# Gate and up projections of the SwiGLU units 1 to 9: tokens stationary instead of weights, and the gated products transposed back on TensorE

## The chip, the cores and the metric

One NeuronCore of a Trainium2 chip runs the whole program; the other cores are idle. The metric is the device time of that core in microseconds, the median of the runs of one kernel. Two changes of a few microseconds are told apart on a program of 2.2 ms only if the runs are close together, so differences of about 0.3% are the limit of what can be read.

## The reference, cut to what matters

The program computes two mixer layers and then four layers of attention and SwiGLU, for 256 tokens of width 1024, in fp32. The change lies in the SwiGLU of the last four layers:

```python
D_FF = -(-8 * D_MODEL // (3 * 256)) * 256          # 2816
def swiglu(h, w_gu, w_down):
    g, u = jnp.split(h @ w_gu, 2, axis=-1)
    return (jax.nn.silu(g) * u) @ w_down
def second_block(...):
    for i in range(DEPTH_2):                        # 4 layers
        ...
        h = modulate(rmsnorm_2(x, norm_gain[i, 1]), sh2, sc2)
        x = x + g2[:, None, :] * swiglu(h, ffn_w_gu[i], ffn_w_down[i])
```

The modulation vectors come from `c_act @ ada_w[i]`, a large weight for a single row, which the kernel computes on VectorE while other work goes on.

## The kernel before, in words

**Three products for one.** Every fp32 operand of a large product is split in two fp32r parts, `hi` and `lo`. `three` issues hi x hi, hi x lo and lo x hi into one accumulation; each has its own weight load.

**The weight stream.** All weights pass in one fixed order through 8 buffers `raw` of 128x1024 fp32, in pieces of 256 rows x 512 columns. SyncE issues the transfers (`h_piece`), each once its buffer was read. ScalarE rounds a piece to `whi` (`h_split`), VectorE takes the difference as `wlo` (`h_rest`). `refill` keeps five split pieces ahead in the code, so in VectorE's queue the rest of a piece stands about four pieces before its use on TensorE. Between them stand pieces of `ada_w`, each multiplied with `c` and added up on VectorE (`h_ada`); most of them fall in the SwiGLU of the second block's layers 0, 1 and 2, and none in that of layer 3. Every fourth of them is followed by four transposes and sums (`ada_sums`). All engines work their queue strictly in the order that the program wrote.

**A SwiGLU layer** (`ffn`) goes through the 2816 hidden columns in 11 units of 256. A unit takes four pieces (`gemm`, K = 1024, columns of gate and of up side by side) and gives the activated product of 256 hidden columns for 256 tokens; two pieces of `w_down` (`down`) then add its share to the output, in four banks of PSUM.

**Unit 0** (`ffn_head`, `h_gu0`) has tokens as stationary operand: a bank holds 128 tokens x (256 gate, 256 up). ScalarE takes tanh of the gate half, VectorE two steps of 256 columns (gated, times up). Its product has tokens on the partitions, and `w_down` needs hidden columns there, so `act_T`, put in `deferred` and taken out by `gemm` after the second piece of the next unit, transposes it with four 128x128 transposes on TensorE (`h_gu0_tr`), and splits it to `OT.hi` on ScalarE and `OT.lo` on VectorE (`h_split_tr`).

**Units 1 to 10** have modes "FF": the weights are stationary and the 256 tokens move, 96 matmuls of 256 columns each. Bank 0 gets the gate, bank 1 the up half, with hidden columns on the partitions, which is what `down` needs. `h_gu`: tanh of 512 on ScalarE, two steps of 512 on VectorE, `OT.hi` on ScalarE, and `OT.lo` on GpSimd (in unit 10 on VectorE).

**The order of a layer**: gemm(v), down(v-1), gemm(v+1), down(v), and so on; unit 8 to 10 of `w_down` are partly held back for the layer's end (`cross`), where the residual, the norm and the next head are interleaved. There are four banks G for the units; two are held by a gemm, one is taken by a transposition, one by the sums of `ada_w`.

Of the kernel before, what the change touches and what calls it, by code (L numbers as in the profile page):

```python
# [7 lines left out]
F32 = mybir.dt.float32  # L8
F32R = mybir.dt.float32r
ALU = mybir.AluOpType  # L10
# [4 lines left out]
D = 1024  # L15
# [410 lines left out]
class Order:  # L426
# [34 lines left out]
    h_gu = h_down = h_down1 = h_last_gain = h_last_rows = h_end = h_none  # L461
# [1519 lines left out]
        self.cross(first, second, N, R, self.ffn_head(l), True)  # L1981
        gb.release(N.nx[0] + N.nx[1])

    def ffn_head(self, l):

        act, made = self.mk_blk(2), []
        self.ffn0 = act, made

        def ev(t, ps, full):
            tmp = self.mk_blk(2)  # L1990
            tanh, gated, u = self.new("ac_ev"), self.new("ve_ev"), self.new("ve_ev")
            self.h_gu0(ps, tmp, act.a[:, t * 256:t * 256 + 256], full, act.w, tanh, gated, u)
            tmp.release([u])
            made.append(u)
            return [u]
        return self.apart(self.HT, ("gu", l, 0), ev)

    def ffn(self, l):
        M, OT = self.M, self.OT
        acc_free = self.slots[0].ps_free + self.slots[1].ps_free  # L2000
        act, made = self.ffn0

        def act_T():
            g, tr = self.gbank(), self.new("pe_tr")
            self.h_gu0_tr(g, act, made, self.gfree[g], tr)
            act.release([tr])
            hi, lo = self.new("ac_tr"), self.new("ve_tr")
            self.h_split_tr(OT.hi[:, 0:2, :].rearrange("p a c -> p (a c)"), OT.lo[:, 0:2, :].rearrange("p a c -> p (a c)"),
                            M.GB[g][:, :], 1.0, tr, OT.waits(0, 2), hi, lo)
            self.gfree[g] = [lo]  # L2010
            OT.write(0, 2, [lo])
        self.deferred.append(act_T)

        def down(v):
            b0 = 2 * (v % 4)
            for kc in range(1 if v == 8 else 2):
                n, lo = self.take(("dn", l, v))
                used = ("pe_w", n)
                self.h_down(b0 + kc, n % NSPL, lo, acc_free if v == 0 and kc == 0 else [], v == 0 and kc == 0, used)
                self.give(n, used)  # L2020
                OT.free[b0 + kc] = [used]

        for v in range(1, 11):
            b0 = 2 * (v % 4)
            tmp = self.mk_blk(4)
            keep = {}

            def ev(g, ps, full):
                if g == 0:
                    keep["g"] = self.new("ve_ev")  # L2030
                    self.h_gu(0, ps[:, :], full, tmp, self.new("ac_ev"), keep["g"], None, None, None, None, False)
                    return [keep["g"]]
                u, hi, lo = self.new("ve_ev"), self.new("ac_ev"), self.new("ve_ev" if v == 10 else "po_ev")
                self.h_gu(1, ps[:, :], full, tmp, None, keep["g"], u, (b0, OT.waits(b0, 2)), hi, lo, v == 10)
                OT.write(b0, 2, [lo])
                keep["r"] = [lo]
                return [u]
            self.gemm(self.HT, 0, ("gu", l, v), D, "FF", ev)
            tmp.release(keep["r"])
            if v == 6:  # L2040
                gb = self.mod_row(l, 40)
            if v == 7 and l in (0, 1):
                w = M.I[("gla_w_in_2", "fox_w_in_2")[l]][0][:, 3072:3088]
                self.narrow_load(w, ("w16a", "w16b")[l])
                if l == 1:
                    self.selb = self.mk_blk(1)
                    self.tsel = self.load("POOL", "sel", self.selb.a[:, 0:16], M.C["foxsel"], self.selb.w)
            if v == 9 and l in (0, 1):
                self.w16[1]()
                if l == 1:  # L2050
                    self.h_sel(self.selb, self.tsel, ("ac_mask", "sel"))
                    self.selb.release([("ac_mask", "sel")])
            if v == 8:
                N = self.modulated(l + 1, 0) if l < 3 else Norm(self, self.row_gain("fn", M.I["final_norm_2"]))
            if v < 10:
                down(v - 1)

        ws = {}
        R = [[Resid(self, gb, u, t, lambda u=u, t=t: M.AB[t][:, u, :], N) for u in range(2)] for t in range(2)]

        def freed(t, u, free):
            self.slots[t].ps_free = free if u == 0 else self.slots[t].ps_free + free

        def part(t, v, u):
            def f():
                for kc in range(v == 8, 2):
                    if (v, kc) not in ws:
                        ws[(v, kc)] = self.take(("dn", l, v))
                    n, lo = ws[(v, kc)]
                    b = 2 * (v % 4) + kc  # L2070
                    done = ("pe_dn", (l, t, v, u, kc))
                    self.h_down1(t, (u,), b, n % NSPL, lo, v == 10 and kc == 1, done)
                    if t == 1 and u == 1:
                        self.give(n, done)
                        OT.free[b] = [done]
                R[t][u].full, R[t][u].free = done, lambda free: freed(t, u, free)
            return f
        if l < 3:
            head = (self.swa_head, self.gla_head, self.fox_head)[(l + 1) % 3](l + 1)
            first = [part(0, v, u) for v in (8, 9) for u in range(2)]  # L2080
            first += [part(0, 10, 0), R[0][0].all, part(0, 10, 1), R[0][1].all]
            second = [part(1, v, u) for v in (8, 9) for u in range(2)] + [part(1, 10, 0)], [], [part(1, 10, 1)]
            self.cross(first, second, N, R, head, False)
            gb.release(N.nx[0] + N.nx[1])
            return None
        yb = self.mk_blk(8)
        stored, tgain = [], self.new("ve_n")
        self.h_last_gain(N.A, tgain)
        for t in range(2):
            F = dict(s=self.smc(2), w=self.smc(6), tmp=[], sq=[], x=[])  # L2090
            for v in (8, 9):
                for u in range(2):
                    part(t, v, u)()
            for i in range(2):
                for kc in range(2):
                    if (10, kc) not in ws:
                        ws[(10, kc)] = self.take(("dn", l, 10))
                    s, lo = ws[(10, kc)]
                    done = ("pe_dn", (l, t, 10, i, kc))
                    self.h_down1(t, (i,), 4 + kc, s % NSPL, lo, kc == 1, done)  # L2100
                    if t and i:
                        self.give(s, done)
                        OT.free[4 + kc] = [done]
                self.last_part(t, i, gb, yb, done, F)
            for u, d in enumerate(self.last_rows(t, N.A, tgain, yb, F)):
                stored.append(self.load("SP", f"out{t}{u}", M.out[0][t * P:t * P + P, u * 512:u * 512 + 512],
                                        yb.a[:, t * D + u * 512:t * D + u * 512 + 512], [d]))
        return stored
# [510 lines left out]
class ScalarE(Order):  # L2619
# [124 lines left out]
            e.wait_ge(*self.at(t))  # L2744
        e.activation(tmp.a[:, 0:256], ps[:, 0:256], ACT.Tanh, scale=0.5).then_inc(*self.up(tanh))

    def h_gu(self, part, ps, full, tmp, tanh, gated, u, dst, hi, lo, end):
        e, OT = self.e, self.OT
        if part == 0:
            e.wait_ge(*self.at(full))  # L2750
# [4 lines left out]
        b0, free = dst  # L2755
# [159 lines left out]
class VectorE(Order):  # L2915
# [289 lines left out]
            e.wait_ge(*self.at(t))  # L3205
        e.scalar_tensor_tensor(act, g, 0.5, ps[:, 256:512], ALU.mult, ALU.mult).then_inc(*self.up(u))

    def h_gu(self, part, ps, full, tmp, tanh, gated, u, dst, hi, lo, end):
        e, OT = self.e, self.OT
        g, up = tmp.a[:, 0:512], tmp.a[:, 512:1024]  # L3210
        if part == 0:
# [5 lines left out]
        for t in tmp.w:  # L3217
            e.wait_ge(*self.at(t))
        e.scalar_tensor_tensor(up, g, 0.5, ps, ALU.mult, ALU.mult).then_inc(*self.up(u))
        if end:  # L3220
            b0 = dst[0]
            e.wait_ge(*self.at(hi))
            e.tensor_tensor(OT.lo[:, b0:b0 + 2, :].rearrange("p a c -> p (a c)"), up,
                            OT.hi[:, b0:b0 + 2, :].rearrange("p a c -> p (a c)").bitcast(F32),
                            ALU.subtract).then_inc(*self.up(lo))

    def h_last_gain(self, fn, done):
        e = self.e
# [230 lines left out]
class GpSimdE(Order):  # L3459
# [37 lines left out]
        e.wait_ge(*self.at(read))  # L3497
        e.tensor_tensor(dst, dst, tmp.a[:, 0:nh * 64], ALU.add).then_inc(*self.up(done))

    def h_gu(self, part, ps, full, tmp, tanh, gated, u, dst, hi, lo, end):  # L3500
        if part == 0 or end:
            return
        e, OT = self.e, self.OT
        b0, free = dst
        e.wait_ge(*self.at(hi))
        e.tensor_tensor(OT.lo[:, b0:b0 + 2, :].rearrange("p a c -> p (a c)"), tmp.a[:, 512:1024],
                        OT.hi[:, b0:b0 + 2, :].rearrange("p a c -> p (a c)").bitcast(F32),
                        ALU.subtract).then_inc(*self.up(lo))


class SyncE(Order):

# [63 lines left out]
```

## Time and profile before

| | us |
|---|---|
| median of 3 runs | 2192.23 (2191.32 to 2197.22) |
| profiled execution, its own time | 2196.12 |
| its span, first to last instruction | 2194.3 |
| TensorE busy in the span | 2138.1 (97%) |
| VectorE | 1568.4 (71%) |
| ScalarE | 1078.7 (49%) |
| GpSimd | 189.4 (9%) |

The mean granted clock of TensorE was 0.994. A share of busy time is a mean over stages: the rows further down show a stage of 156 us each for the SwiGLU of three layers. In the timelines the second number is an instruction's duration, from issue to the end of its last result; matmuls overlap, so what a matmul costs the stream is the distance between two starts, not its duration. Some matmul records can be missing from a trace.

### The profile page before, as it was taken

The page shows a single profiled execution, that of the slowest core. Times are in us where ns is not written, and L with a number is a line of the kernel's source. Part 1 is how long each engine was busy: PE and PEld are TensorE (multiplying, and loading weights), DVE is VectorE, ACT ScalarE, POOL GpSimd, SP SyncE. Part 2 cuts the span into 40 slices and gives each one's busy share as a digit, 9 for nine tenths or more (in the row PEclk, how much of TensorE's full clock was granted, in tenths as well). Part 3 has the DMA queues.
Part 4 walks back from the last instruction along what each step waited for, and adds up shares of the span by engine and source line. Part 5 has one row for each costly group of instructions (what it writes and reads, how often), then busy time and mean ns, then how long its engine had stood idle before and what let it go on. Part 6 is the DMA issues. An engine that isn't in the chain of part 4 may idle for free. (4 is left out here: it accounts for less than half of the span.)

```text
span 2194.3 us, 34064 instructions
## 1 busy us (share of the span) xinstructions
PE 2138.1 (97%) x13639; PEld 1904.5 (87%) x13639; DVE 1568.4 (71%) x2168; ACT 1078.7 (49%) x2087; POOL 189.4 (9%) x242
## 2 busy tenths in 40 slices
PE   8999999999999999999999998999999999999998
PEld 7999888879988888777999787999898899778997
DVE  6578657766776677667899677899745896657545
ACT  5454555544545564455445443454545455455433
POOL 1101001101010011010001001001000001010000
PEclk9999999999999999999999999999999999999999
DMA  9887645577786455633999444699644697535662
GB/s 300 290 267 243 223 147 158 174 234 227 251 269 205 138 168 182 216 112 120 314 346 358 160 135 144 234 360 364 227 138 144 233 358 253 165 102 177 197 205 75
DMA packets 297284, 472.47 MB, mean 215 GB/s; under 512 B 20241, under 2 KB 153051, under 8 KB 297126
## 3 DMA queue, kind: packets, MB, share of 16 engines
q1 hardware_dynamic: 286566, 440.68, 60.2%
q0 software_dynamic: 10560, 29.61, 4.6%
q8 instruction: 108, 1.77, 0.3%
q14 instruction: 50, 0.41, 0.1%
HBM read 465.36 MB, written 4.85 MB: 214 GB/s over the span
## 5 line engine op out<-in xcount | busy, mean ns | idle before, releaser
L150 DVE TENSOR_TENSOR wlo<-raw,whi 128x1024 fp32r<-128x1024 f32 x640 | 769.6, 1232 | 202.5 <-ACT whi L144 200.9
L144 ACT ACTIVATE whi<-raw 128x1024 fp32r<-128x1024 f32 x640 | 645.7, 1056 | 158.3 <-DMA raw<-in_ffn_w_gu 72.3
L138 PE MATMUL G<-HTh,whi 128*128 128x256 f32 x2336 | 671.7, 288 | 9.4 <-ACT pool L144 7.0
L138 PE MATMUL G<-HTh,wlo 128*128 128x256 f32 x2336 | 662.0, 283 | 0.0
L138 PE MATMUL G<-HTl,whi 128*128 128x256 f32 x2336 | 661.8, 283 | 0.0
L138 PEld LDWEIGHTS G<-HTh,whi 128*128 128x128 f32 x2336 | 448.7, 192 | 18.2 <-issue 10.6
L138 PEld LDWEIGHTS G<-HTl,whi 128*128 128x128 f32 x2336 | 448.9, 192 | 2.1
L138 PEld LDWEIGHTS G<-HTh,wlo 128*128 128x128 f32 x2336 | 448.6, 192 | 0.0
L144 ACT ACTIVATE pool<-G 128x128 f32<-128x128 f32 (+2 forms) x400 | 165.1, 433 | 533.2 <-PE G L138 473.7
L138 PE MATMUL G<-whi,HTh 128*128 128x512 f32 (+1 forms) x784 | 313.7, 400 | 9.3 <-ACT HTh L144 8.7
L138 PE MATMUL G<-whi,HTl 128*128 128x512 f32 (+1 forms) x784 | 304.1, 388 | 6.1 <-DVE HTl L158 6.1
L138 PE MATMUL G<-wlo,HTh 128*128 128x512 f32 (+1 forms) x784 | 302.2, 385 | 0.0
L158 DVE SCALAR_TENSOR_TENSOR pool<-raw,c,pool 128x512 f32<-128x512 f32 x336 | 270.5, 805 | 8.1 <-DMA raw<-in_ada_w 0.6
L158 DVE SCALAR_TENSOR_TENSOR pool<-pool,G 128x512 f32<-128x512 f32 (+1 forms) x140 | 91.6, 655 | 163.0 <-ACT pool L144 131.3
L138 PEld LDWEIGHTS G<-whi,HTl 128*128 128x128 f32 x784 | 149.1, 190 | 42.8 <-DVE HTl L158 13.2
L138 PEld LDWEIGHTS G<-whi,HTh 128*128 128x128 f32 x784 | 149.3, 190 | 42.2 <-issue 9.0
L138 PEld LDWEIGHTS G<-wlo,HTh 128*128 128x128 f32 x784 | 149.7, 191 | 25.7
L138 PE MATMUL A<-whi,OTh 128*128 128x512 f32 x352 | 138.2, 393 | 1.4 <-DVE wlo L150 1.4
L138 PE MATMUL A<-wlo,OTh 128*128 128x512 f32 x352 | 137.5, 391 | 0.0
L138 PE MATMUL A<-whi,OTl 128*128 128x512 f32 x352 | 137.0, 389 | 0.0
L138 PE MATMUL G<-whi,OTh 128*128 128x512 f32 x272 | 109.7, 403 | 0.9 <-DVE HTl L158 0.9
L138 PE MATMUL G<-whi,OTl 128*128 128x512 f32 x272 | 106.4, 391 | 0.0
(194 smaller groups left out, 2253.4 us busy)
## 6 DMA issues: line engine op xcount, KB each, us to landing
raw<-in_ada_w SPq DMA_DIRECT2D x192, 512.0 KB, 6.2
raw<-in_ffn_w_gu SPq DMA_DIRECT2D x352, 256.0 KB, 5.1
raw<-in_w_in SPq DMA_DIRECT2D x128, 512.0 KB, 4.6
raw<-in_ffn_w_down SPq DMA_DIRECT2D x88, 512.0 KB, 6.9
raw<-in_w_in SPq DMA_DIRECT2D x160, 256.0 KB, 4.6
raw<-in_swa_w_in SPq DMA_DIRECT2D x24, 512.0 KB, 4.4
pool<-mod_rows POOLq DMA_DIRECT2D x24, 512.0 KB, 6.4
raw<-in_gla_w_in SPq DMA_DIRECT2D x24, 512.0 KB, 4.9
```

The lines of the kernel that those rows point to most:

```text
L138: return self.e.matmul(out, a, b, start=start, stop=stop, skip_group_check=True) if self.e else self
L144: return self.e.activation(out, a, func, bias=bias, scale=scale, accum_out=accum) if self.e else self
L150: return self.e.tensor_tensor(out, a, b, op) if self.e else self
L158: return self.e.scalar_tensor_tensor(out=out, in0=a, scalar=s, in1=b, op0=op0, op1=op1) if self.e else self
```

## The change: what it does

Units 1 to 9 now go as unit 0: modes "TT", 48 matmuls with 128 tokens stationary and 512 weight columns moving, two banks of 128 tokens each; two tanh of 256, four VectorE steps of 256, and `turned`, the old `act_T` for every unit, which transposes the product of unit v in the middle of unit v+1. `OT.lo` of these units comes from VectorE, read from PSUM. Unit 10 stays as it was (`last_unit`). GpSimd has no part in the SwiGLU any more.

```diff
-    def ffn_head(self, l):
+    def gated_rows(self):
         act, made = self.mk_blk(2), []
-        self.ffn0 = act, made
         def ev(t, ps, full):
             tmp = self.mk_blk(2)
 ...
+        return act, made, ev
+    def ffn_head(self, l):
+        act, made, ev = self.gated_rows()
+        self.ffn0 = act, made
         return self.apart(self.HT, ("gu", l, 0), ev)
 ...
+        def turned(v, act, made):
+            def f():
+                g, tr, b0 = self.gbank(), self.new("pe_tr"), 2 * (v % 4)
+                self.h_gu0_tr(g, act, made, self.gfree[g], tr)
+                act.release([tr])
+                hi, lo = self.new("ac_tr"), self.new("ve_tr")
+                self.h_split_tr(OT.hi[:, b0:b0 + 2, :].rearrange("p a c -> p (a c)"),
+                                OT.lo[:, b0:b0 + 2, :].rearrange("p a c -> p (a c)"),
+                                M.GB[g][:, :], 1.0, tr, OT.waits(b0, 2), hi, lo)
+                self.gfree[g] = [lo]
+                OT.write(b0, 2, [lo])
+            self.deferred.append(f)
+        turned(0, *self.ffn0)
 ...
-            self.gemm(self.HT, 0, ("gu", l, v), D, "FF", ev)
-            tmp.release(keep["r"])
+        for v in range(1, 11):
+            if v < 10:
+                act, made, ev = self.gated_rows()
+                self.gemm(self.HT, 0, ("gu", l, v), D, "TT", ev)
+                turned(v, act, made)
+            else:
+                last_unit()
 ...
 class GpSimdE:
-    def h_gu(self, part, ps, full, tmp, tanh, gated, u, dst, hi, lo, end):
-        ...
-        e.tensor_tensor(OT.lo[...], tmp.a[:, 512:1024], OT.hi[...].bitcast(F32), ALU.subtract)
```

## Rows read from the trace of the kernel before

**Rows 1.** Part 1 of the page: busy time, share, instructions by engine.
```profile
PE 2138.1 (97%) x13639; PEld 1904.5 (87%) x13639; DVE 1568.4 (71%) x2168; ACT 1078.7 (49%) x2087; POOL 189.4 (9%) x242
```
**Rows 2.** Busy time by engine in the SwiGLU of layers 0, 1, 2; clock, DMA share, GB/s.
```profile
1055.00:1211.00 156.00, 156.00 (x1124) 147.84 (x1123) 143.49 (x176) 76.97 (x169) 15.45 (x14) 1.00 1.00 348
1398.00:1554.00 156.00, 156.00 (x1122) 147.75 (x1122) 146.56 (x179) 77.42 (x171) 15.56 (x15) 1.00 1.00 350
1729.00:1885.00 156.00, 154.61 (x1104) 145.83 (x1104) 120.92 (x142) 71.78 (x137) 15.97 (x16) 1.00 0.87 300
```
**Rows 3.** Chain that ended last, layer 3 (start, us, what): one gemm, one down.
```profile
2044.74 11.51 PE G L138 x96
2056.25 5.47 PE A L138 x24
```
**Rows 4.** Timeline of TensorE, mixer stage (start, us, engine, line, tiles, shapes): 24, 4 and 12 in line.
```profile
390.94 0.39 PE L138 MATMUL G<-whi,HTh 128*128 128x512 f32 x1
...
396.38 0.60 PE L141 MATMUL A<-ident_t,S 128*128 128x128 f32 x4
396.74 0.47 PE L138 MATMUL G<-whi,HTh 128*128 128x512 f32 x1
...
399.57 1.05 PE L138 MATMUL A<-pool,W 128*128 128x128 f32 x8
```
**Rows 5.** Timeline of TensorE: unit 1 of layer 3 behind its transposes; eight transposes, layer 2.
```profile
2015.94 0.60 PE L141 MATMUL G<-ident_t,pool 128*128 128x128 f32 x4
...
2022.13 0.40 PE L138 MATMUL A<-whi,OTh 128*128 128x512 f32 x1
...
1774.86 1.03 PE L141 MATMUL G<-ident_t,pool 128*128 128x128 f32 x8
1775.65 0.36 PE L138 MATMUL G<-HTh,whi 128*128 128x256 f32 x1
```
**Rows 6.** Timelines of VectorE, GpSimd, TensorE, SwiGLU of layer 1, one unit's end.
```profile
1451.92 1.47 DVE L158 SCALAR_TENSOR_TENSOR pool<-pool,G 128x512 f32<-128x512 f32 x2
1453.31 0.15 DVE L150 TENSOR_TENSOR mod<-sm,adb 128x4 f32<-128x4 f32 x1
1453.38 2.60 DVE L158 SCALAR_TENSOR_TENSOR pool<-raw,c,pool 128x512 f32<-128x512 f32 x2
...
1464.52 1.53 DVE L158 SCALAR_TENSOR_TENSOR pool<-raw,c,pool 128x512 f32<-128x512 f32 x2
...
1454.13 1.30 POOL L150 TENSOR_TENSOR OTl<-pool,OTh 128x512 fp32r<-128x512 f32 x1 [16.47 <-ACT OTh L144]
...
1468.13 0.40 PE L138 MATMUL A<-whi,OTh 128*128 128x512 f32 x1
```
**Rows 7.** Instructions of one line in 1398 to 1554 us: ns min/median/max.
```profile
L158 DVE SCALAR_TENSOR_TENSOR pool<-raw,c,pool x83: 739/751/1890, 1400.3 to 1536.9; 128x512 f32<-128x512 f32 x83
```
**Rows 8.** Timelines of VectorE and ScalarE: unit 0 of layers 1 and 2.
```profile
1387.54 0.87 DVE L158 SCALAR_TENSOR_TENSOR pool<-pool,G 128x256 f32<-128x256 f32 x2
1388.33 1.22 DVE L150 TENSOR_TENSOR wlo<-raw,whi 128x1024 fp32r<-128x1024 f32 x1
...
1386.31 0.39 ACT L144 ACTIVATE pool<-G 128x256 f32<-128x256 f32 x1 [0.70 <-PE G L138]
...
1723.89 0.69 DVE L158 SCALAR_TENSOR_TENSOR OTl<-G,OTh 128x512 fp32r<-128x512 f32 x1 [3.61 <-ACT OTh L144]
1724.50 0.48 DVE L155 TENSOR_SCALAR pool<-raw,c 128x512 f32<-128x512 f32 x1
```
**Rows 9.** Timelines of TensorE and VectorE, layer 2, late units; last bracket: idle before.
```profile
1799.46 0.40 PE L138 MATMUL A<-whi,OTh 128*128 128x512 f32 x1
...
1812.25 0.63 PE L141 MATMUL G<-ident_t,pool 128*128 128x128 f32 x4 [0.98 <-DVE pool L158]
...
1813.30 0.39 PE L138 MATMUL G<-HTh,whi 128*128 128x256 f32 x1 [0.41 <-DVE wlo L150]
...
1801.51 0.48 DVE L155 TENSOR_SCALAR pool<-raw,c 128x512 f32<-128x512 f32 x1
```

More of the change, by code:

```diff
@@ L2000, in ffn @@
         acc_free = self.slots[0].ps_free + self.slots[1].ps_free
[L2001 to L2012, printed above, removed]
+        def turned(v, act, made):
[11 more added lines that the diff above has]
+        turned(0, *self.ffn0)
         def down(v):
@@ L2021, in down, with last_unit @@
                 OT.free[b0 + kc] = [used]
[L2023 to L2026, printed above, removed]
+        def last_unit():
+            tmp, keep, b0 = self.mk_blk(4), {}, 4
             def ev(g, ps, full):
@@ L2030, in ev @@
                     keep["g"] = self.new("ve_ev")
-                    self.h_gu(0, ps[:, :], full, tmp, self.new("ac_ev"), keep["g"], None, None, None, None, False)
+                    self.h_gu(0, ps[:, :], full, tmp, self.new("ac_ev"), keep["g"], None, None, None, None)
                     return [keep["g"]]
-                u, hi, lo = self.new("ve_ev"), self.new("ac_ev"), self.new("ve_ev" if v == 10 else "po_ev")
-                self.h_gu(1, ps[:, :], full, tmp, None, keep["g"], u, (b0, OT.waits(b0, 2)), hi, lo, v == 10)
+                u, hi, lo = self.new("ve_ev"), self.new("ac_ev"), self.new("ve_ev")
+                self.h_gu(1, ps[:, :], full, tmp, None, keep["g"], u, (b0, OT.waits(b0, 2)), hi, lo)
                 OT.write(b0, 2, [lo])
@@ L2037, in ev @@
                 return [u]
-            self.gemm(self.HT, 0, ("gu", l, v), D, "FF", ev)
+            self.gemm(self.HT, 0, ("gu", l, 10), D, "FF", ev)
             tmp.release(keep["r"])
+        for v in range(1, 11):
[5 more added lines that the diff above has]
+                last_unit()
             if v == 6:
@@ L2745, in h_gu0, with h_gu @@
         e.activation(tmp.a[:, 0:256], ps[:, 0:256], ACT.Tanh, scale=0.5).then_inc(*self.up(tanh))
-    def h_gu(self, part, ps, full, tmp, tanh, gated, u, dst, hi, lo, end):
+    def h_gu(self, part, ps, full, tmp, tanh, gated, u, dst, hi, lo):
         e, OT = self.e, self.OT
@@ L3206, in h_gu0, with h_gu @@
         e.scalar_tensor_tensor(act, g, 0.5, ps[:, 256:512], ALU.mult, ALU.mult).then_inc(*self.up(u))
-    def h_gu(self, part, ps, full, tmp, tanh, gated, u, dst, hi, lo, end):
+    def h_gu(self, part, ps, full, tmp, tanh, gated, u, dst, hi, lo):
         e, OT = self.e, self.OT
@@ L3219, in h_gu @@
         e.scalar_tensor_tensor(up, g, 0.5, ps, ALU.mult, ALU.mult).then_inc(*self.up(u))
[L3220 to L3225, printed above, removed]
+        b0 = dst[0]
+        e.wait_ge(*self.at(hi))
+        e.tensor_tensor(OT.lo[:, b0:b0 + 2, :].rearrange("p a c -> p (a c)"), up,
+                        OT.hi[:, b0:b0 + 2, :].rearrange("p a c -> p (a c)").bitcast(F32),
+                        ALU.subtract).then_inc(*self.up(lo))
     def h_last_gain(self, fn, done):
@@ L3498, in h_rope @@
         e.tensor_tensor(dst, dst, tmp.a[:, 0:nh * 64], ALU.add).then_inc(*self.up(done))
[L3500 to L3508, printed above, removed]
 class SyncE(Order):
```

## The prediction

> **What bounds the kernel now.** The busy times come first: TensorE 2138.1 of 2194.3 us, everything else far below [rows 1]. A mean hides stages, so the second view is the SwiGLU of the layers. In those of layers 0 and 1 TensorE is busy in all of 156.00 us at a granted clock of 1.00 (the 2.4 GHz level), but VectorE is nearly full as well, 143.49 and 146.56 us, and in layer 2 TensorE loses 1.4 us [rows 2]. Third comes the chain that ended last, in layer 3, where no `ada_w` pieces come: it consists of TensorE's gemm and down in turn, 11.51 us for 96 matmuls and 5.47 us for 24 [rows 3]. A unit is thus 16.98 us of nothing but TensorE. So a cheaper unit shortens the program directly in layer 3, and elsewhere only as long as VectorE, which comes next, keeps up.
>
> **The matmuls.** 11.51 us for 96 is 119.9 ns for 256 columns [rows 3]. The trace has the other form, tokens stationary and 512 columns moving, in the mixers: 24 of them from 390.94 to 396.38 us, 5.44 us or 226.7 ns each, with no wait in between [rows 4]. The columns are the same in number; the time that goes is 2 x 119.9 - 226.7 = 13 ns for each matmul saved. A unit of 48 costs 10.88 us, 0.63 less; 36 units (9 in each of four layers) give 22.7 us. The down behind it is now preceded by its own form and should take 5.44 instead of 5.47 us [rows 3, 4], 36 x 0.03 = 1.1 us.
>
> **The transposes.** Each of the 36 units adds four. Between 512-column streams four take 0.36 us, and the 12 matmuls behind them 2.83 us where half of 5.44 is 2.72: 0.47 us in all [rows 4]. In the 256-column form, unit 1 of layer 3, transposes and half a unit take 6.19 us against 5.76 without: 0.43 us [rows 5]. Joined to four of `ada_sums` the second four still cost 0.79 - 0.36 = 0.43 [rows 4, 5]. 32 stand in 512-column units (15.0 us), 4 in unit 10 (1.7), and the four of unit 0 change surroundings (4 x 0.04 = 0.2): 16.9 us. They don't wait for their input, which is finished some 2 us behind the unit's end, while down and half the next unit, 10.9 us, stand before them. The bounds for a set are 0.36 (nothing lost behind) and 0.58, the above with 0.11 more on re-entry; 0.47 is the row in the right surroundings.
>
> **TensorE's sum**: 22.7 + 1.1 - 16.9 = 6.9 us, or 0.19 a unit.
>
> The Trainium skill speaks against this change. "TensorE: Matmul & The Clock Gate", section "Back-to-back issue gap", gives N/2.4 + 2.5 ns for a matmul. By that 96 would take 10.48 us and 48 would take 10.36, 0.12 us saved where a transposition costs more, so that the kernel would be some 11 us slower. The rows show 13 ns for each matmul where the page has 2.5, and a measurement decides.
>
> **ScalarE** changes one tanh of 512 columns for two of 256, 0.39 us each [rows 8], and takes `OT.hi` from PSUM; at half load [rows 2] this is free. It no longer stands before `OT.hi` until VectorE has finished.
>
> **VectorE.** Before: two steps of 512, 1.39 us from 1451.92 to 1453.31 [rows 6]. After: two pairs of 256, 0.79 us a pair [rows 8]. There is a catch in the code: `ev` gives its scratch block back at once, so the second half takes the same block and its tanh waits for the first half's last step. Where VectorE is late, it stands idle for that tanh, 0.39 and some 0.06 of handover [rows 8]. A late unit costs 0.87 + 0.45 + 0.79 = 2.10, 0.71 more than before; an early one 0.2 more. `OT.lo` adds 0.61 (1723.89 to 1724.50) [rows 8]. That is +1.32 us a unit on an engine with 9 to 12 us to spare in 9 units [rows 2].
>
> Against it stands what GpSimd no longer does. Its `OTl` step ran for 1.30 us from 1454.13; the pair of VectorE steps that began at 1453.38 took 2.60 us, while the like pair at 1464.52 took 1.53: 1.07 us lost [rows 6]. It shows too in the longest such step, 1890 ns beside a median of 751 [rows 7]. I take it that one blocks the other, and that the 1.07 us come back in each dense unit: VectorE's net is +0.25. The Trainium skill has this in "SBUF — State Buffer", section "Who interferes with whom": a VectorE instruction with two inputs in SBUF contends with a GpSimd instruction that reads SBUF; the trace agrees with its 1.07 us, and it raises my trust in the relief.
>
> **The new wait.** `OT.lo` of unit v now stands in VectorE's queue behind the second piece of down(v), about four splits and their `ada_w` steps after unit v's end, and down(v) waits for it. Behind it in the queue are the splits of the next unit. In layer 1 the place is 1464.52 us, the step would end at 1465.2, and down starts at 1468.13 [rows 6]: 2.9 us to spare. A dense unit uses up 0.25 + 0.19 = 0.44 of it, seven units 3.1, while unit 1, where VectorE isn't late, gives 1.3 back (0.8 by the earlier pair and 1.07 by GpSimd, less 0.61). So no stall in layer 1, and less pressure in layer 0. In layer 2 the place is 1801.51 and down starts at 1799.46 [rows 9]. By then four GpSimd steps (-4.3), three late pairs (+2.1), unit 1's pair (-0.8) and three earlier `OT.lo` (+1.8) move it by -1.2: ready at 1801.0, TensorE there at 1798.7, a new stall of 2.3 us. But TensorE waited just behind anyway, at 1812.25 and 1813.30 [rows 9], for the same VectorE. From 1801.0, 5.44 + 5.44 + 0.79 + 0.11 us lead to 1812.8 against 1813.30 before: 0.5 us gained at this point where the plain count has 1.0 for five units. So 0.5 us goes.
>
> **Sum**: 6.9 - 0.5 = 6.4 us. The profiled execution has a span of 2194.3 and a time of 2196.12; the median of the runs is 2192.23. I expect a span near 2187.9 and a median of **2185.8 us**.
>
> **Rivals.**
> *Slower: VectorE becomes the bound in layers 0 to 2.* If the relief from GpSimd doesn't come, a dense unit loses 1.32 + 0.19 = 1.5 us. Layer 1 then stalls 7 x 1.5 - 2.9 = 7.6 us, layer 0, where VectorE has 3 us more to spare, some 5, layer 2 about 5: 17.6 - 6.9 gives +10.7, 2203 us. The point from which it decides is a relief of about half: at 0.5 us a unit the stalls are 3.8 + 0.6 + 2.5 and eat the 6.9. For it: VectorE's load [rows 2]. Against it: rows 6 and 7. Chance 0.09.
> *Queue order.* VectorE arrives at the new step before `OT.hi` is there (transposes, 0.6 us of latency, 0.6 of ScalarE) and loses 0.5 us in each dense unit too. Then layer 1 stalls 7 x 0.94 - 2.9 = 3.7, layer 0 0.4, layer 2 1 more: 2190.9 us. For it: a strict queue that must now meet TensorE twice in a unit. Against it: a late VectorE arrives late. Chance 0.21.
> *The transposes cost only themselves*, 0.36: 32 x 0.11 = 3.5 us more gained, 2182.3 us. For it: the loss on re-entry might lie under a longer matmul. Against: 2.83 [rows 4]. Chance 0.09.
> *The fixed part of a matmul isn't saved*, as the page's rule has it: if a 256-column matmul in these units cost half of 226.7, TensorE would only lose 16.9 us, 2209 us; 11.51 us for 96 excludes it [rows 3]. Chance 0.01.
> The forecast keeps 0.60.
>
> **Range and chances.** 0.3% is 6.6 us, about what a measurement of this kernel can tell from no change; the line is at 2185.6, at my forecast. The forecast's own spread is about 1.5 us each way, a little more of it on the small side, since small waits cost and none pays: 0.28 faster, 0.32 same. The cheap transposes are faster (0.09), the queue order is the same by this measure (0.18) with a part slower (0.01) or faster (0.02), the first and last rival are slower (0.10). Together 0.39 faster, 0.50 same, 0.11 slower. The range of 2182 to 2193 takes in the cheap transposes and the queue order and leaves out the slow cases.
>
> **What would show it.** Right: units of layer 3 of 16.8 us, made of 10.9 + 0.47 + 5.44; the long 1.8 us steps of VectorE gone; GpSimd busy 36 x 1.3 = 47 us less; in layer 2 a wait of TensorE for `OTl` of about 2 us before a down, and the later waits for `acc` and `wlo` gone. Wrong: waits for `OTl` or `wlo` in layers 0 and 1; matmuls of 512 columns above 227 ns in the units; more than 0.5 us for four transposes; VectorE's idle time before `OTl`, put down to ScalarE, in the dense units.

## The result, and the profile after

The changed kernel takes 2218.59 us (median of 4 runs, 2216.23 to 2218.93), the kernel before 2194.32 beside it: a ratio of 1.0116, with an interval of 1.0104 to 1.0129. It is slower by 24 us where 6.4 us of gain were forecast, and outside the range. The profiled execution took 2218.57 us with a span of 2216.8, against 2196.12 and 2194.3 before; the mean granted clock is 0.992, before 0.994.

The first view is the page: busy time by engine and, from its fifth part, the PE transposes into G by the program's `ident_t` with the idle time before them and what ended it.

```profile
PE 2137.9 (96%) x12055; PEld 1831.8 (83%) x12055; DVE 1579.2 (71%) x2276; ACT 1080.3 (49%) x2123; POOL 141.3 (6%) x206
...
L141 PE MATMUL G<-ident_t,pool 128*128 128x128 f32 x645 | 95.9, 281 | 33.5 <-DVE OTl L158 23.3
```

1584 instructions of TensorE are gone [rows 1], 1728 matmuls less and 144 transposes more, and its busy time didn't fall by the 6.9 us of the count: some of the matmuls that are left ran slower. GpSimd does 48.1 us less. The second line is where the time went: TensorE stood idle for 23.3 us in front of transposes until VectorE had written `OTl`. No such wait was there before, and none was forecast before a transposition.

The second view answers [rows 2]: the SwiGLU of layers 0, 1 and 2 and the last one, each from its first down to the end of its last (in layer 3, the fourth line, to the start of its last block of downs), busy time by engine, then granted clock, DMA share and GB/s.

```profile
1054.00:1229.00 175.00, 169.73 (x827) 142.06 (x826) 154.10 (x219) 83.87 (x188) 3.16 (x5) 0.99 0.92 316
1401.00:1581.00 180.00, 171.27 (x825) 142.99 (x825) 156.64 (x222) 84.45 (x189) 3.70 (x6) 0.98 0.91 313
1742.00:1924.00 182.00, 170.22 (x813) 142.07 (x811) 135.79 (x184) 79.43 (x155) 3.83 (x7) 0.97 0.79 265
2046.00:2195.00 149.00, 149.00 (x722) 125.42 (x721) 82.37 (x96) 62.08 (x80) 0.00 (x0) 1.00 0.52 166
```

Measured between the same downs of both kernels, these stretches changed from 169.3, 169.3, 169.6 and 150.1 us to 175.1, 180.3, 181.9 and 149.1. That is +5.8, +11.0, +12.3 and -1.0, together 28.1; everything between the stretches is 5.6 us shorter (2.2 of it in unit 1, before the first down, 0.55 in each layer; the other 3.4 lie outside the changed work, and they are no gain: all that lies outside the stretches takes 1577.8 us in the profiled execution before, which was a long one, and 1573.9 and 1573.7 in those of e3 and e4 below, two kernels whose instructions there are the same or nearly so). 28.1 - 5.6 is the 22.5 us between the two spans. VectorE is no fuller than before, and TensorE now has idle time in the three stages that had next to none.

The layer without `ada_w`, layer 3, has what was forecast. TensorE's timeline there (start, duration, then the instruction): one unit, its transposes in the middle, its down, and the next unit.

```profile
2051.11 0.39 PE L138 MATMUL G<-whi,HTh 128*128 128x512 f32 x1
...
2056.55 0.60 PE L141 MATMUL G<-ident_t,pool 128*128 128x128 f32 x4
2056.91 0.48 PE L138 MATMUL G<-whi,HTh 128*128 128x512 f32 x1
...
2062.48 0.39 PE L138 MATMUL A<-whi,OTh 128*128 128x512 f32 x1
...
2067.92 0.39 PE L138 MATMUL G<-whi,HTh 128*128 128x512 f32 x1
```

24 matmuls take 5.44 us, the four transposes 0.36, the 24 behind them 5.57 (0.13 lost on re-entry), the down 5.44: 16.81 us. Before it was 11.51 + 5.47 [rows 3]. So the gain is real, and it is eaten elsewhere.

**Where it is eaten.** One slot of layer 1, TensorE first, then ScalarE and VectorE of the same microseconds (the bracket is the idle time before, and what ended it):

```profile
1428.52 1.03 PE L141 MATMUL G<-ident_t,pool 128*128 128x128 f32 x8
1431.75 0.66 PE L141 MATMUL G<-ident_t,pool 128*128 128x128 f32 x4 [2.19 <-DVE OTl L158]
...
1433.23 0.63 PE L138 MATMUL G<-whi,HTh 128*128 128x512 f32 x1
...
1433.66 0.63 PE L138 MATMUL G<-wlo,HTh 128*128 128x512 f32 x1
...
1429.16 0.60 ACT L144 ACTIVATE OTh<-G 128x512 fp32r<-128x512 f32 x1 [2.68 <-PE G L141]
...
1429.87 1.22 DVE L150 TENSOR_TENSOR wlo<-raw,whi 128x1024 fp32r<-128x1024 f32 x1
1431.01 0.69 DVE L158 SCALAR_TENSOR_TENSOR OTl<-G,OTh 128x512 fp32r<-128x512 f32 x1
```

Here twelve transposes stand in the middle of a unit: four of `turned`, and two sets of `ada_sums`. There are four banks G. Two are held by the gemm. `turned` takes the third, the first set of sums the fourth, and for the second set `gbank` hands out the oldest bank that nobody holds: the one that `turned` filled a moment ago, free only when ScalarE has made `OTh` from it and VectorE `OTl`. TensorE, being in order, waits for both with all of the unit's second half behind it. Before, the two sets of sums had the two free banks to themselves, the eight transposes of [rows 5].

There are eleven such waits: 1.38, 1.07 and 2.00 us in layer 0; 2.19, 1.85, 1.85 and 2.00 in layer 1; 5.96, 1.90, 2.12 and 0.97 in layer 2. They add up to the 23.3 of the page. The transposes of the sums don't read `OTl`: only the bank from which VectorE makes it ties them to it. A second loss stands behind the longer ones, in the granted clock: the same columns as above, for the wait at 1431.75 and behind it.

```profile
1428.00:1432.00 4.00, 1.81 (x14) 1.41 (x13) 3.96 (x6) 2.57 (x10) 0.00 (x0) 1.00 1.01 355
1432.00:1436.00 4.00, 4.00 (x14) 3.22 (x13) 3.93 (x6) 2.09 (x9) 0.00 (x0) 0.57 1.07 377
1436.00:1440.00 4.00, 4.00 (x18) 3.27 (x18) 1.47 (x4) 0.84 (x3) 0.00 (x0) 1.00 1.06 386
```

Behind the wait the clock goes to its lower level, 1.2 GHz: matmuls of 512 columns start 0.43 us apart (1433.23 and 1433.66), and the 24 behind the transposes take 7.16 us instead of 5.57. That happens behind five of the eleven waits (2.00, 2.19, 2.00, 5.96 and 2.12 us) and costs some 7.5 us in all; behind the 1.85 at 1507.27 the clock stayed at 1.00.

From its first transposition to the next matmul, each of the eleven groups of twelve takes 2.42 to 7.76 us where 1.22 would do (0.79 for eight and 0.43 for four more), 26.5 us too much; with the 7.5 us of the clock that is 34.0. Against it stand 1.8 us of old waits in layer 2 that are gone (before, eight transposes, the first four at 1810.68 and the rest at 1812.25, led to the next matmul at 1813.30 [rows 9]: 2.62 us where 0.79 would do) and some 1.0 us of gain in each of four layers between the downs: 34.0 - 1.8 - 4.0 = 28.2, and 28.1 were measured.

### The profile page after: what moved, and what is told of

It reads as the page before. It is cut to its first block, busy times and chain, and to the rows that moved or that the text cites. A ratio compares the mean times of both kernels' runs of the same rounds, so it can differ in the third digit from the quotient of the medians.

```text
span 2216.8 us, 30997 instructions
## 1 busy us (share of the span) xinstructions
PE 2137.9 (96%) x12055; PEld 1831.8 (83%) x12055; DVE 1579.2 (71%) x2276; ACT 1080.3 (49%) x2123; POOL 141.3 (6%) x206
## 4 chain that ended last, share of the span: by engine, by line
PE 77%; DVE 13%; issue 6%; ACT 3%; DMA 1%; POOL 0%; SPq 0%; ACTq 0%; DVEq 0%; POOLq 0%
PE G L138 61%; PE A L138 13%; DVE pool L158 7%; DVE wlo L150 3%; PE G L141 3%; ACT pool L144 2%; PE A L141 1%; DVE pool L150 1%; DMA pool<-mod_rows 1%; DVE X L150 1%; DVE OTl L158 1%; ACT whi L144 1%; DVE pool L155 0%; POOL sm L150 0%; DVE HTl L158 0%
## 5 line engine op out<-in xcount | busy, mean ns | idle before, releaser
L138 PE MATMUL G<-whi,HTh 128*128 128x512 f32 (+1 forms) x1360 | 543.1, 399 | 10.0 <-ACT HTh L144 9.4
L138 PE MATMUL G<-whi,HTl 128*128 128x512 f32 (+1 forms) x1360 | 530.7, 390 | 6.1 <-DVE HTl L158 6.1
L138 PE MATMUL G<-wlo,HTh 128*128 128x512 f32 (+1 forms) x1360 | 528.4, 389 | 0.0
L144 ACT ACTIVATE pool<-G 128x128 f32<-128x128 f32 (+3 forms) x436 | 171.4, 411 | 520.6 <-PE G L138 428.5
L138 PE MATMUL G<-HTh,whi 128*128 128x256 f32 x1184 | 344.2, 291 | 9.0 <-ACT pool L144 7.0
L138 PE MATMUL G<-HTh,wlo 128*128 128x256 f32 x1184 | 336.4, 284 | 0.0
L138 PE MATMUL G<-HTl,whi 128*128 128x256 f32 x1184 | 336.3, 284 | 0.0
L138 PEld LDWEIGHTS G<-HTh,whi 128*128 128x128 f32 x1184 | 228.1, 193 | 16.0 <-issue 10.6
L138 PEld LDWEIGHTS G<-HTl,whi 128*128 128x128 f32 x1184 | 228.2, 193 | 0.7
L138 PEld LDWEIGHTS G<-HTh,wlo 128*128 128x128 f32 x1184 | 228.0, 193 | 0.0
L141 PE MATMUL G<-ident_t,pool 128*128 128x128 f32 x645 | 95.9, 281 | 33.5 <-DVE OTl L158 23.3
```

Source lines behind the costliest of these rows:

```text
L138: return self.e.matmul(out, a, b, start=start, stop=stop, skip_group_check=True) if self.e else self
L141: return self.e.transpose(out, a, ident) if self.e else self
L144: return self.e.activation(out, a, func, bias=bias, scale=scale, accum_out=accum) if self.e else self
```

## The experiments

Two theories were put against each other. A, the bank: the second set of sums shares the bank of the transposition. B, VectorE: it is full, `OTl` comes late in its queue, and the waits are only the place where that shows. By A the waits go when the sums are parted, with VectorE as full as it was; by B they don't.

**e2_sum_later: part the two sets of sums.** This is the changed kernel with the edit in SwiGLU units 1 to 10 alone (`spared` is 1 there and 0 elsewhere). The number of instructions on each engine stays.

```diff
             if kk == 2:
-                self.ada_sums(4, 0)
+                self.ada_sums(4, self.spared)
+            if kk == 4 and self.spared:
+                self.ada_sums(4, 0)
```

With one bank to be left free, one set of sums is taken after the second piece and the other goes behind the first piece of the unit's second half.

> The changed kernel, with one difference: in the units of the SwiGLU at most one set of ada_w sums is put in the middle of a unit, and a second that is due comes one piece (2.7 us) later. Theory A (bank): in the changed kernel the second set of sums takes the very PSUM bank that the new transposes have just filled, and TensorE waits for OTl; 11 such places cost about 27 us of gaps and 7 us of matmuls at half clock behind them. Then the waits for OTl before transposes go or shrink to under 3 us in all, and the kernel comes out between 2184 and 2192 us, at or below the kernel before. Theory B (VectorE is too full in layers 0 to 2, rival 1 of the prediction): the waits only move to wlo or to OTl before a down; the kernel stays above 2203 us.

**e3_before_sum_later** is the same edit in the kernel before, to see what the moving itself does.

> The kernel before with the same later place for the second set of ada_w sums: a control. Both theories: within 0.2% of the kernel before, since there no bank was short.

Measured: e2 2196.9 us against 2194.41, 1.0017 (1.0008 to 1.0025). Another order of the sums gives back 22 of the 24 us. It is less than A had set: 2184 to 2192 us, and under 3 us of waits for `OTl`. e3 2193.8, 0.9997 (0.9988 to 1.0006): in the kernel before, the edit is worth nothing. So the bank is what the change added. (No run left the sums in their place and gave them a further bank; all of them move instructions in time.) The stretches of e2 take 170.3, 171.5, 174.3 and 149.1 us. 8.4 us of waits for `OTl` are left, 4.8 of it one wait in layer 2, where `OTl` is so late that even the set moved back meets it. Timelines of e2, TensorE, then ScalarE and VectorE:

```profile
1781.88 1.11 PE L141 MATMUL G<-ident_t,pool 128*128 128x128 f32 x4 [4.76 <-DVE OTl L158]
...
1775.90 0.58 ACT L144 ACTIVATE OTh<-G 128x512 fp32r<-128x512 f32 x1
...
1781.14 0.68 DVE L158 SCALAR_TENSOR_TENSOR OTl<-G,OTh 128x512 fp32r<-128x512 f32 x1
```

`OTh` is there at 1776.5 and VectorE comes to `OTl` 4.7 us later, behind splits and `ada_w` steps that stand before it in its queue. This is B's mechanism, inside A's: lateness makes a shared bank dear.

**e4_before_lo_dve: the step from GpSimd to VectorE alone.** Of the kernel before, nothing transposed:

```diff
-                u, hi, lo = self.new("ve_ev"), self.new("ac_ev"), self.new("ve_ev" if v == 10 else "po_ev")
-                self.h_gu(1, ..., hi, lo, v == 10)
+                u, hi, lo = self.new("ve_ev"), self.new("ac_ev"), self.new("ve_ev")
+                self.h_gu(1, ..., hi, lo, True)
```

> The kernel before with one part of the change alone: OTl of units 1 to 9 on VectorE instead of GpSimd. If GpSimd's step blocked VectorE for 1.07 us a unit, VectorE's long steps (1.8 us beside 0.75) vanish, its busy time in 1398 to 1554 us changes by 9 x (0.69 - 1.07) = -3.4 us, and the time is within 0.15% of before or up to 2 us less (layer 2). If there is no relief, VectorE's load grows by 9 x 0.62 = 5.6 us in that stretch, and layers 1 and 2 stall, +3 us or more.

Measured: 2197.27 us, 1.0013 (1.0004 to 1.0023). The rows are the `ada_w` steps of layer 1 (ns min, median, max), the busy times of 1395 to 1551 us, and `OTl` in layer 1 with the idle time before it:

```profile
L158 DVE SCALAR_TENSOR_TENSOR pool<-raw,c,pool x83: 743/751/754, 1398.9 to 1536.1; 128x512 f32<-128x512 f32 x83
...
1395.00:1551.00 156.00, 156.00 (x1123) 147.66 (x1122) 143.16 (x188) 76.99 (x171) 3.90 (x6) 1.00 0.99 348
...
L150 DVE TENSOR_TENSOR OTl<-pool,OTh 128x512 fp32r<-128x512 f32 x9 | 6.2, 693 | 6.3 <-ACT OTh L144 6.3
```

The long steps of up to 1890 ns [rows 7] are gone, and VectorE does nine steps of 0.69 us more in 3.4 us less busy time (143.16 against 146.56 [rows 2]). So GpSimd did hold VectorE up, by (3.4 + 6.2) / 9 = 1.07 us a unit, the forecast's figure. What that gives, the queue takes back: VectorE waits 6.3 us for `OTh`. And layer 2 grows by 1.7 us; the median is 2.9 us above the kernel before, and where the rest arises isn't shown. The Trainium skill's page "SBUF — State Buffer", section "Who interferes with whom", has the contention; its size is in these rows alone.

**e5_scratch: e2, and a scratch block for each half.** The two halves of an evacuation no longer share `tmp`.

```diff
         def ev(t, ps, full):
-            tmp = self.mk_blk(2)
+            if not tmps:
+                tmps[:] = [self.mk_blk(2), self.mk_blk(2)]
+            tmp = tmps.pop()
```

> The kernel with the later sum, and a scratch block of its own for each half of a unit, so that the second tanh doesn't wait for the first half's last VectorE step. Expected: VectorE's idle time of 0.45 us between the halves in the late units goes (27 units in layers 0 to 2, about 8 us in the listing of idle time by ScalarE); the time falls by 0 to 2 us against the kernel with the later sum alone, all in layer 2. If VectorE is the bound in layers 0 and 1 too (theory B), it falls by 5 us or more.

Measured: 2192.62, 0.9994 (0.9985 to 1.0003). The stretches are 170.2, 170.3, 172.0 and 149.1; it is 4.3 us faster than e2, and level with the kernel before. Neither theory had that: A said 0 to 2 us, all in layer 2, B 5 or more, and layer 1 gives 1.2 and layer 2 2.3. So how late VectorE is counts wherever TensorE still has to wait for it; 6.4 us of waits for `OTl` are left. The bubble that was forecast is in the changed kernel's VectorE timeline, a pause of 0.51 us for the second tanh:

```profile
1420.13 0.88 DVE L158 SCALAR_TENSOR_TENSOR pool<-pool,G 128x256 f32<-128x256 f32 x2 [0.51 <-ACT pool L144]
```

**e7_scratch_only** has the scratch blocks and the sums as in the changed kernel.

> The changed kernel with a scratch block of its own for each half, the sums where the change has them. It takes 0.5 us of VectorE's idle time out of each late unit and leaves the bank shared. Theory A: the waits for OTl before the second set of sums stay, shorter where VectorE is late; 2212 to 2217 us. Theory B: VectorE is the bound, 27 units x 0.5 us come back and the time falls below 2206 us.

Measured: 2220.31, 1.0125 (1.0112 to 1.0139), level with the changed kernel and some 3 us above what was expected. Waits for `OTl` are still 24.7 us, but not the same ones. The blocks are from the same ring as those of the transfer of modulation rows, and the new order makes ScalarE wait for it, and VectorE for ScalarE (ScalarE, then VectorE; it comes again at 1537.41 in layer 1):

```profile
1185.41 0.66 ACT L144 ACTIVATE pool<-G 128x256 f32<-128x256 f32 x2 [3.58 <-DMA mod_rows<-pool]
...
1185.83 1.21 DVE L158 SCALAR_TENSOR_TENSOR pool<-pool,G 128x256 f32<-128x256 f32 x3 [2.74 <-ACT pool L144]
```

The last wait for `OTl` of layer 0 and that of layer 1 stand behind these two places: they grew from 2.00 and 2.00 us to 4.22 and 4.80. The other nine shrank from 19.3 to 15.7 us in all, as A had it. So the blocks took VectorE's bubble away and put a wait for a transfer in its place, and this run doesn't price the bubble alone. (In e5 too, such a wait of ScalarE, 3.59 and 3.66 us, stands ahead of two of the three waits for `OTl` that are left.) B's figure, below 2206 us, stays far off even without the two.

**e6_turn_early: e5, and the transposition one piece earlier.** In units 2 to 10 `deferred` is taken out after the first piece, so `OTl` gets 2.7 us more; and a bank that the sums give back keeps its age (`gbank` hands out the free bank of the lowest age), so that the next unit takes it and not one that was emptied just before.

```diff
-            if kk == 2 and self.deferred:
+            if kk == (0 if self.spared == 2 else 2) and self.deferred:
...
-                self.gfree[g], ..., self.gage[g], ... = [added], ..., max(self.gage) + 1, ...
+                self.gfree[g], ... = [added], ...
+                if not self.spared:
+                    self.gage[g] = max(self.gage) + 1
```

> The changed kernel with the later second sum and a scratch block for each half, and now the transposes of unit v after the first piece of unit v+1 instead of the second (unit 0 as before), and the bank of a set of sums keeps its age, so that the next unit takes it instead of one that was emptied just before. The bank of the transposes has then 5.4 us instead of 2.7 until the second set of sums wants it. Theory A (bank): the waits for OTl left over (3.4 us in layer 2, 1.5 us in layers 0 and 1) go, layers 0 and 1 come to 168.7 us, layer 2 to about 169, and the time is 2187 to 2190 us, ratio 0.997 to 0.998 to the kernel before. Theory B (VectorE too full): waits for wlo in their place, layer 2 stays above 171 us, ratio 0.9994 as before this step.

Measured: 2188.43 us against 2193.18, 0.9976 (0.9965 to 0.9986), so 4.8 us faster than the kernel before and some 30 faster than the change as it was made. 0.24% is little, but the interval lies wholly below 1. The stretches are 168.9, 169.0, 169.3 and 149.1. Busy times of the first three (columns as above), and all waits for `OTl` left, two in layer 2:

```profile
1054.68:1223.62 168.94, 168.12 (x828) 140.51 (x827) 153.25 (x219) 84.14 (x188) 3.16 (x5) 1.00 0.93 328
1395.34:1564.29 168.95, 168.12 (x829) 140.51 (x827) 155.70 (x222) 85.05 (x189) 3.70 (x6) 1.00 0.96 334
1723.54:1892.81 169.27, 166.66 (x812) 138.73 (x811) 134.62 (x184) 79.89 (x155) 3.84 (x7) 1.00 0.84 285
...
1773.75 0.66 PE L141 MATMUL G<-ident_t,pool 128*128 128x128 f32 x4 [0.91 <-DVE OTl L158]
...
1792.62 0.55 PE L141 MATMUL G<-ident_t,pool 128*128 128x128 f32 x3 [0.88 <-DVE OTl L158]
```

B falls by these rows as a cause of the 24 us: VectorE does the same work (219, 222 and 184 instructions in both kernels, 443.6 us busy here and 446.5 there), it is 92% busy in layer 1, and TensorE waits 1.8 us for it in all. What VectorE's lateness does is to set how dear each shared bank is.

**e9_early_no_ages** is e6 without the kept ages.

> The kernel with the transposes after the first piece, without the other half of that step: a bank of sums is the youngest again when it is given back. It tells which half took the waits away. If it was the time that the bank of the transposes has until the second set of sums, this kernel has the same layer times, 168.9, 168.9 and 169.3 us within 0.5, and a ratio of 0.997 to 0.9985. If it was the order of the banks, the waits for OTl of 1.5 us in layers 0 and 1 and of 3.4 us in layer 2 are back, or waits for a bank at the start of a unit, and the ratio is 0.9990 to 1.0000.

Measured: 2190.76 against 2192.7, 0.9986 (0.9977 to 0.9995); stretches 169.4, 170.0, 169.4 and 149.1, waits for `OTl` 1.8 us as in e6. The earlier transposition is what removes them. Layer 1 and the ratio lie just outside what was expected of that reading (168.9 within 0.5, and 0.9985). The ages are worth about 1 us, two short waits for a bank at the start of unit 10 (0.20 and 0.82 us, until VectorE has read unit 9); the intervals of e6 and e9 overlap, so more can't be said of them.

**e8_before_ages: the kernel before with the parted sums and kept ages.** A control.

> The kernel before with the order of sums and banks of the last kernel (a second set of sums one piece later, ages kept): a control for how much of that kernel's time has nothing to do with the form of the units. Both theories: 0.9990 to 1.0005 of the kernel before.

Measured: 2208.24, 1.0063 (1.0049 to 1.0077). No theory gave that. Timelines of e8 at the start of unit 10 in layer 1, TensorE, then ScalarE:

```profile
1547.48 0.55 PE L138 MATMUL G<-HTh,whi 128*128 128x256 f32 x1 [3.66 <-ACT pool L144]
...
1550.18 0.41 PE L138 MATMUL G<-HTh,whi 128*128 128x256 f32 x1
1550.39 0.41 PE L138 MATMUL G<-HTl,whi 128*128 128x256 f32 x1
...
1545.68 0.63 ACT L144 ACTIVATE OTh<-pool 128x512 fp32r<-128x512 f32 x1 [2.20 <-DVE pool L158]
1546.22 0.26 ACT L144 ACTIVATE pool<-G 128x128 f32<-128x128 f32 x1
```

It is the same fault with the roles turned round. With kept ages the next unit gets the two banks of the sums, and it needs both with its first matmuls. ScalarE hasn't yet read the later sums: in its queue they stand behind `OTh`, which waits for VectorE. The unit waits 3.66 us, with the lower clock behind it (0.21 us between matmuls of 256 columns); layers 0 and 2 have one such wait each, 2.41 and 3.15 us. In e6 no `OTh` stands there, since ScalarE makes it from the transposes in the middle of a unit: the sums of the same slot are read by 1536.85, and unit 10 starts at 1537.95 without a wait.

## Why the prediction was wrong, point by point

*Matmuls: right.* A unit's 48 matmuls and its down take 10.88 and 5.44 us, as worked out from [rows 3, 4]. The formula that the prediction took from the Trainium skill ("TensorE: Matmul & The Clock Gate", "Back-to-back issue gap") would have had layer 3 longer; it is 1.0 us shorter. That section gives it for a matmul by itself and says that it counts too little for few columns, so it was a weaker witness against the change than the prediction made of it.

*Transposes: right in size.* 0.49 us a set in a unit of 512-column matmuls, where 0.47 was taken. The unit of layer 3 is 16.81 us, forecast 16.8.

*Relief from GpSimd: right*, 1.07 us a unit by e4.

*Scratch block: right*, 0.51 against the 0.45 taken; it is worth 4 us in e5 against e2. In the changed kernel its worth stays open, since e7 brought a wait for a transfer with it.

*The wait of down(v) in layer 2, 2.3 us: not seen.* TensorE is stopped at the transposes already, half a unit ahead of it, and what VectorE is late by is paid there.

***The step that failed*** is "Joined to four of `ada_sums` the second four still cost 0.79 - 0.36 = 0.43". It was drawn from the eight transposes of [rows 5], which are two sets of sums. It prices the time of TensorE and not the bank. Those very rows show both free banks in use. In eleven of the units of layers 0 to 2 a third set comes with the change, and the description of the kernel (two banks for a gemm, one for a transposition, one for the sums) fits a slot with one set of sums only. The term of 0.43 us measured, in these slots, 2.8 us on average (0.43 + 26.5 / 11), and 3.5 with the clock. The error is 11 x 3.1 = 34 us, against some 6 forecast as gain. I had looked for a wait of TensorE in front of what is new, the transposes of `turned`, whose input is early; the wait came in front of what stood there before.

*The rival "queue order"* had the right kind of thing, VectorE and TensorE meeting twice in a unit, with a chance of 0.21. It was priced as VectorE's lost time against the spare time before down(v), 3 us. In fact its queue is read from the other side. Even with VectorE on time, the chain takes about 1 us of TensorE's time. It is plain at the shortest waits, 0.97 and 1.07 us, where VectorE goes to `OTl` 0.73 us behind the start of `OTh`. Timelines of the changed kernel, TensorE, ScalarE, VectorE:

```profile
1153.07 1.03 PE L141 MATMUL G<-ident_t,pool 128*128 128x128 f32 x8
1155.17 0.66 PE L141 MATMUL G<-ident_t,pool 128*128 128x128 f32 x4 [1.07 <-DVE OTl L158]
...
1153.70 0.60 ACT L144 ACTIVATE OTh<-G 128x512 fp32r<-128x512 f32 x1 [4.19 <-PE G L141]
...
1154.43 0.69 DVE L158 SCALAR_TENSOR_TENSOR OTl<-G,OTh 128x512 fp32r<-128x512 f32 x1
```

Eleven times 1 us, with the 3.2 us that the starts and stops around the waits cost (26.5 - 23.3), are 14 us, more than the 6.4 of gain. The other 20 (12.3 us of waits and 7.5 of the clock) come where VectorE reaches `OTl` later still. This split is worked out from the shortest waits, no run had a VectorE that was always on time; that both parts hang on the shared bank is what e2 and e6 show.

*The first rival*, VectorE as the bound: it named the right direction and under half the size (+10.7 us) for a reason that isn't there. VectorE's relief came, and its busy time is nearly the same in the kernels that wait and in those that don't. (Its threshold has a slip: at a relief of 0.5 us layer 1 would stall 7 x 1.01 - 2.9 = 4.2 us, not 3.8; nothing hangs on it.)

*The chances.* 0.11 for slower was too little. Each user of a resource that the change adds (engine time, queue place, scratch block) had its line in the sum but one, the bank, and that line was missing from the rivals too.

## What to carry to other kernels

When a change adds a user to a pool of buffers or banks, list for each slot of the schedule who holds which, and look at the fullest slot, not the usual one: a pool that is one short costs the whole release chain through other engines' queues, not the added work. The costs of an inserted step are read where its neighbours stand too: what comes behind it on the in-order engine is what waits. And a change that fails by this can be sound: with the sums parted from it, scratch to itself and an earlier place, the same change was 4.8 us faster than the kernel before, not 24 slower.

## What the runs showed of the hardware that was not expected

A stall of TensorE can cost more than its own length. Behind the wait of 2.19 us in front of 1431.75 the granted clock of the next 4 us was 0.57, and 24 matmuls took 7.16 us instead of 5.57; the five cases cost 1.2 to 1.6 us each on top of waits of 2.0 to 6.0. Behind the other six, of 0.97 to 1.90 us, the 24 matmuls took 5.55 to 5.57.

Transposition sets are dearer apart than joined, by little: a unit with one, two and three sets apart takes 16.80, 17.29 and 17.78 us in e6, 0.49 each, and 17.21 with two joined in the changed kernel. The 0.49 is 0.36 for four transposes and 0.13 for getting back into the stream.
